# Dilated and sparse attention heads scaled one group later, the output and the mixers' rotation reordered

## The chip, the cores and the metric

One core of a Trainium2 chip runs the whole program in one launch. Its engines are TensorE (PE, with its weight loads, PEld), VectorE (DVE), ScalarE (ACT), GpSimd (POOL) and SyncE (SP), which issues the loads of the weights. The metric is the device time in microseconds, lower is better. Each time is the median of several executions.

## The reference

Two transformer stacks run one after the other on 256 tokens of width 1024, in float32. The first has two layers (the mixers, each with a feed-forward part behind it); it matters here for its rotary embedding of the grouped and the latent heads. The second has a layer with a recurrent mixer beside four sparse block heads, then a layer of eight dilated heads, each followed by an MLP. The parts that the change touches, cut short:

```python
# sparse heads (4 heads of 128, one block of 128 tokens and the selected past block)
s_own = where(causal, q k_own * Dh**-0.5, NEG);  s_sel = where(valid, q k_sel * Dh**-0.5, NEG)
p = softmax(concat([s_sel, s_own]));  out = p_sel v_sel + p_own v_own
# dilated heads (8 heads of 128, three window and stride pairs g)
s = where(mask_g, q_g k * Dh**-0.5, NEG);  lse_g = logsumexp(s)
o = sum_g softmax(lse)_g * (exp(s - lse_g) v)
x = layer_norm(alpha * x + o @ w_out)
# rotary embedding of q and k, before the scores
concat([x1 * c - x2 * s, x1 * s + x2 * c])
```

With 256 tokens all three groups of a dilated head can share one sum of exponentials: the kernel adds the three masked exponentials and multiplies by one reciprocal.

## The kernel before

**Data flow.** Weights come from memory in units of up to 128x2048 numbers. SyncE loads a unit into a ring of three (`wraw`), waiting for the low part of the unit three before. ScalarE rounds it (`split_hi`, L310, ring of four `whi`), VectorE takes the rest (`split_lo`, L318, ring of three `wlo`), and waits before it until TensorE has finished the unit three before. TensorE multiplies each block three times: high by high, high by low, low by high (L378 to L381 for a tile of a projection, 24 multiplications; L456 to L459 for row blocks). `ahead_dve` makes the splits two units ahead of TensorE, at the step where a unit begins; `ahead_act` works three ahead.

**Order.** Each engine walks the same list of steps, written out in Python, and does its own part of each step in that order. An engine never does a later step while it waits in an earlier one. So the list sets what stands behind what. Semaphores count each result.

**Attention of the dilated and the sparse heads.** A head goes through these parts: `scores` on TensorE (L2501 and L2502, or L1671 and L1672); on VectorE `masked_dve` (L917: add the mask, keep the least value); on ScalarE `scores_act` (L974: exponentials with their sums); for the dilated heads GpSimd adds the second group (`scores_pool`, L990). Then `weights_dve` on VectorE: two sums of two numbers (L942, L944), the third group's sum (L946), reciprocal (L950), scaling (L956). Two heads later TensorE transposes the weights (`headturn`, L1001), ScalarE copies them (L1011), and one more head later TensorE multiplies by the values (`values`, L1022), ScalarE and VectorE split the result (L1028, L1033). Before the change `scores_dve` does `masked_dve` and `weights_dve` in one step.

**Rotation.** For dilated and sparse heads four projected tiles are a group. ScalarE copies each tile (L848) and its 32 rotated rows (L851). TensorE permutes them (`four_pe`, L839), VectorE finishes (`four_dve`, L861, L862 and four times L867). It is called at the first tile of the next group; `qend` and `qk_end` do it for the last group. In the mixers `rot_act` swaps rows in four copies (L797) and `turn_dve` multiplies and adds (L806, L807, L810); there `rot_dve` first makes the split of tile j and then turns tile j-1.

**Steps around the heads.** `Dilated` deals its projections (`qk`, `v`) between the heads by `due`; `wo` steps are quarter row blocks of the output projection with the first four heads, six multiplications each. `Rwkv` mixes its recurrence's preparation (`prep`), late projection tiles (`z`) and the sparse heads (`att`). A z tile passes ScalarE (L1708), GpSimd (L1744) and VectorE (L1725). GpSimd also multiplies and adds the norm's gains (L723, L717) behind each of the first four dilated heads' L990.

## Time and profile before

| What | Value |
|---|---|
| Median of 3 executions | 1636.87 us (1635.64 to 1637.04) |
| The profiled execution's own time | 1636.17 us |
| Its span in the trace | 1634.4 us |
| TensorE busy | 1583.4 us, 97% |
| VectorE busy | 1113.0 us, 68% |
| ScalarE busy | 936.9 us, 57% |
| GpSimd busy | 301.2 us, 18% |
| Mixers with their feed-forward parts | 0 to about 880 us |
| Recurrent layer with the sparse heads | about 880 to 1090 us |
| Its MLP | about 1090 to 1280 us |
| Dilated heads | about 1280 to 1445 us |
| Last MLP | about 1445 us to the end |

The busy times overlap. What counts is where TensorE stands still, and what it waits for there. Rows of the timeline begin with the start in us from the span's start and the duration in us; a bracket at the end gives the engine's idle time just before and who ended it.

### The profile page before, as it was taken

The numbers are of one execution on the slowest core, as the hardware profiler recorded it, in microseconds if no ns is written. First come the engines' busy times: TensorE is split into PE (matmuls) and PEld (weight loads), VectorE is DVE, ScalarE is ACT, GpSimd is POOL, SyncE is SP. The second block draws the span as 40 slices with busy tenths as digits, with TensorE's granted clock in tenths as the row PEclk, the third lists the DMA queues.
The fourth block names the chain that finished last, engine by engine and source line by source line (L and its number), as shares of the span: only waits on it lengthen the run. The fifth ranks groups of instructions, "written<-read, shape, count | busy, mean of one in ns | idle before, by whom it ended". The sixth has DMA issues, their size and how long they took to land. (4 is left out here: it accounts for less than half of the span.)

```text
span 1634.4 us, 28813 instructions
## 1 busy us (share of the span) xinstructions
PE 1583.4 (97%) x11908; PEld 1433.5 (88%) x11908; DVE 1113.0 (68%) x1751; ACT 936.9 (57%) x1510; POOL 301.2 (18%) x218
## 2 busy tenths in 40 slices
PE   7999999999999999999999998889999999899998
PEld 6999998999899999999988986768888889878886
DVE  5575656887466665668855686579844778779744
ACT  5777755765458776556644664346533656545531
POOL 0000210433000002104320252016500021008300
PEclk9999999999999999999999999999999999999999
DMA  9344454575543534636654633025665535345651
GB/s 293 129 148 133 143 197 170 194 245 174 193 179 105 168 117 155 218 130 207 205 177 167 232 112 104 30 80 204 210 227 182 205 107 177 108 179 179 235 185 73
DMA packets 45394, 272.78 MB, mean 167 GB/s; under 512 B 4816, under 2 KB 9040, under 8 KB 16208
## 3 DMA queue, kind: packets, MB, share of 16 engines
q1 hardware_dynamic: 44544, 266.23, 47.6%
q10 hardware_dynamic: 720, 4.72, 0.8%
q8 instruction: 94, 1.54, 0.4%
q14 instruction: 36, 0.29, 0.1%
HBM read 269.88 MB, written 1.05 MB: 166 GB/s over the span
## 5 line engine op out<-in xcount | busy, mean ns | idle before, releaser
L318 DVE TENSOR_TENSOR b_wlo<-b_wraw,b_whi 128x2048 fp32r<-128x2048 f32 (+1 forms) x263 | 569.7, 2170 | 175.1 <-PE b_ps L459 125.3
L310 ACT ACTIVATE b_whi<-b_wraw 128x2048 fp32r<-128x2048 f32 (+1 forms) x263 | 467.8, 1779 | 200.0 <-PE b_ps L459 147.1
L378 PE MATMUL b_ps<-b_H,b_whi 128*128 128x256 f32 x1784 | 505.3, 283 | 0.2 <-ACT b_four L851 0.2
L380 PE MATMUL b_ps<-b_H,b_whi 128*128 128x256 f32 x1784 | 498.0, 279 | 0.0
L381 PE MATMUL b_ps<-b_H,b_wlo 128*128 128x256 f32 x1784 | 498.0, 279 | 0.0
L378 PEld LDWEIGHTS b_ps<-b_H,b_whi 128*128 128x128 f32 x1784 | 335.3, 188 | 9.4 <-issue 8.2
L380 PEld LDWEIGHTS b_ps<-b_H,b_whi 128*128 128x128 f32 x1784 | 335.5, 188 | 0.6
L381 PEld LDWEIGHTS b_ps<-b_H,b_wlo 128*128 128x128 f32 x1784 | 335.3, 188 | 0.0
L424 PE MATMUL b_ps<-b_H,b_whi 128*128 128x512 f32 x448 | 155.7, 390 | 0.0
L1550 POOL TENSOR_TENSOR b_fl<-b_ab,b_fh 128x256 fp32r<-128x256 f32 x44 | 93.7, 2129 | 213.7 <-ACT b_fh L1523 213.7
L425 PE MATMUL b_ps<-b_H,b_wlo 128*128 128x256 f32 x448 | 126.3, 282 | 0.0
L456 PE MATMUL b_ps<-b_whi,b_gh 128*128 128x512 f32 x256 | 99.7, 389 | 0.0
L459 PE MATMUL b_ps<-b_whi,b_gl 128*128 128x512 f32 x256 | 99.6, 389 | 0.0
L457 PE MATMUL b_ps<-b_wlo,b_gh 128*128 128x512 f32 x256 | 99.6, 389 | 0.0
L424 PEld LDWEIGHTS b_ps<-b_H,b_whi 128*128 128x128 f32 x448 | 84.1, 188 | 17.6
L1620 POOL TENSOR_TENSOR b_gl<-b_relu,b_gh 128x256 fp32r<-128x256 f32 x64 | 71.6, 1129 | 126.3 <-ACT b_gh L1592 126.3
L1472 POOL TENSOR_TENSOR b_mg<-b_mg,b_scr 128x256 f32<-128x256 f32 x32 | 31.5, 984 | 291.6 <-DVE b_scr L1455 291.6
L425 PEld LDWEIGHTS b_ps<-b_H,b_wlo 128*128 128x128 f32 x448 | 84.7, 189 | 0.1
L974 ACT ACTIVATE b_S<-b_S,b_small 128x256 f32<-128x256 f32 (+1 forms) x116 | 54.9, 475 | 42.1 <-DVE b_small L917 30.0
L456 PE MATMUL b_ps<-b_whi,b_H 128*128 128x512 f32 x160 | 64.8, 405 | 9.5 <-DVE b_wlo L318 6.2
L456 PE MATMUL b_ps<-b_whi,b_fh 128*128 128x512 f32 x176 | 68.7, 390 | 0.0
L459 PE MATMUL b_ps<-b_whi,b_fl 128*128 128x512 f32 x176 | 68.5, 389 | 0.0
(365 smaller groups left out, 2711.5 us busy)
## 6 DMA issues: line engine op xcount, KB each, us to landing
b_wraw<-in_w SPq DMA_DIRECT2D x223, 1024.0 KB, 4.9
b_wraw<-in_w SPq DMA_DIRECT2D x37, 512.0 KB, 3.5
b_bias<-in_rpb SPq DMA_DIRECT2D x8, 512.0 KB, 10.9
b_gains<-in_gains ACTq DMA_DIRECT2D x4, 1024.0 KB, 5.0
b_wraw<-in_w SPq DMA_DIRECT2D x2, 768.0 KB, 4.3
b_X<-in_x SPq DMA_DIRECT2D x2, 512.0 KB, 6.1
b_cA<-in_cA SPq DMA_DIRECT2D x2, 512.0 KB, 8.6
out<-b_X SPq DMA_DIRECT2D x4, 256.0 KB, 2.1
```

The lines of the kernel that those rows point to most:

```text
L310: e.activation(whi[u % NHI][:, 0:n], raw[u % NRAW][:, 0:n], ACT.Copy).then_inc(up("w_hi", "whi", u))
L318: e.tensor_tensor(wlo[u % NLO][:, 0:n], raw[u % NRAW][:, 0:n], hi.bitcast(F32), ALU.subtract).then_inc(up("w_lo", "wlo", u))
L378: e.matmul(out, wh, x.hi[:, kk, :], start=k == 0, stop=False)
L380: e.matmul(out, wh, x.lo[:, kk, :], start=False, stop=False)
L381: ins = e.matmul(out, wl, x.hi[:, kk, :], start=False, stop=last)
L424: e.matmul(bank[:, :], part(u, ng * P, k, gi * P, gi * P + P, False), H2[:, k, :, :].rearrange("p s t -> p (s t)"), start=k == 0, stop=False)
L425: ins = e.matmul(bank[:, 0:T], part(u, ng * P, k, gi * P, gi * P + P, True), x.hi[:, k, :], start=False, stop=k == job.nk - 1)
L456: e.matmul(out, xh, part(u, n, q, 0, n, False), start=k == 0, stop=False)
L457: e.matmul(out, xh, part(u, n, q, 0, n, True), start=False, stop=False)
L459: ins = e.matmul(out, xl, part(u, n, q, 0, n, False), start=False, stop=k == job.nk - 1)
L1550: e.tensor_tensor(self.f.lo[:, m, :], self.ab[p % 4][:, 0, :], self.f.hi[:, m, :].bitcast(F32), ALU.subtract).then_inc(up("f_lo", self.f.k ...
L1620: e.tensor_tensor(self.f.lo[:, j, :], self.r[p % 4][:, :], self.f.hi[:, j, :].bitcast(F32), ALU.subtract).then_inc(up("f_lo", self.f.key, ...
```

## The change

It separates `masked_dve` and `weights_dve` in the dilated and sparse heads, so that other VectorE steps stand between them. In the dilated list, `weights` stands half a head's projections later, and around head 7 the last rotation, the output steps and their splits are reordered. In the sparse part the projection tiles come in the order Q0 Q1 K0 K1 Q2 Q3 K2 K3, head 0's scores go ahead of z tile 12, the weights of a head are made in the step of the next, and the ring of score buffers starts at another buffer. In the mixers each tile is turned in its own step, so the last one (`rot` 5) ahead of the split of `vg`.

```diff
--- before.py
+++ after.py
@@ -812,8 +812,7 @@
 
     def rot_dve(e, w, job, j, tn, place):
         ahead_dve(e, w, job, j)
-        if j:
-            turn_dve(e, w, job, j - 1, tn, place)
+        turn_dve(e, w, job, j, tn, place)
 
 
 
@@ -889,10 +888,6 @@
             for what in h["needs"]:
                 w.wait_ge(*at(*what))
             h["qk"][g](e, bank).then_inc(banks.full((a.key, "s", i, g)))
-
-    def scores_dve(e, w, a, i):
-        masked_dve(e, w, a, i)
-        weights_dve(e, w, a, i)
 
     def masked_dve(e, w, a, i):
         h, k = a.heads[i], a.key
@@ -1419,10 +1414,8 @@
                     rot_dve(e, w, self.rot, *i, self.tn, self.place)
                 elif what == "vg":
                     ahead_dve(e, w, self.vg, 0)
-                    turn_dve(e, w, self.rot, 5, self.tn, self.place)
             for j in range(2):
                 rot_dve(e, w, self.uqr, j, self.tn, self.place_uq)
-            turn_dve(e, w, self.uqr, 1, self.tn, self.place_uq)
             for j in range(4):
                 ahead_dve(e, w, self.uq, j)
             for j in range(4):
@@ -1622,6 +1615,8 @@
 
 
     class Rwkv:
+        TILES = [0, 1, 4, 5, 2, 3, 6, 7]
+
         def __init__(self, key):
             H = Split(Hh, Hl, key, True)
             with ExitStack() as s1:
@@ -1635,7 +1630,7 @@
                     self.lora = sb(s2, "lora", [P, 3, 512])
                     self.mid, self.end, self.hst = sb(s2, "mid", [P, 4, 4]), sb(s2, "end", [P, 4, 4]), sb(s2, "hst", [P, 16])
                     self.cM = sb(s2, "cM", [P, sum(w for _, w in atM.values())])
-                    S_ring = [self.Z[:, 12:14, :].rearrange("p a t -> p (a t)")[:, 0:384]] + ring(s2, "S", 2, [P, 384])
+                    S_ring = ring(s2, "S", 2, [P, 384]) + [self.Z[:, 12:14, :].rearrange("p a t -> p (a t)")[:, 0:384]]
                     T_ring = [spare[:, 0:384], sb(s2, "T", [P, 384])]
                     small = sb(s2, "small", [P, 6, 12])
                     self.Q, self.K, self.V = sb(s2, "moQ", [P, 4, T]), sb(s2, "moK", [P, 4, T]), sb(s2, "moV", [P, 2, 512])
@@ -1644,7 +1639,8 @@
                         o, w = atM[name]
                         return self.cM[:, o:o + w]
 
-                    self.qk = Job("moqk", "ab_w_in_2", 0, range(8), pieces(1824, 2848), H)
+                    heads_of = pieces(1824, 2848)
+                    self.qk = Job("moqk", "ab_w_in_2", 0, range(8), [heads_of[t] for t in self.TILES], H)
                     self.tn = Gathering("moba", s2, CM("cos2"), CM("sin2"), CM("perm2"), ("cM",), scr[2:4], [self.qk])
                 with ExitStack() as s3:
                     self.BKt, self.RKB = sb(s3, "BKt", [P, 4, 512]), sb(s3, "RKB", [P, 2, 2, 4, 2, 64])
@@ -1671,19 +1667,20 @@
                     e.matmul(ps[:, 0:P], self.Q[:, h, 0:P], self.K[:, h, 0:P], start=True, stop=True)
                     return e.matmul(ps[:, P:P + T], self.Q[:, h, P:T], self.K[:, h, :], start=True, stop=True)
                 heads.append(head(qk=[qk], masks=[[cz[:, 0:P], cz[:, T:2 * T]]], widths=[P, T], tables=[("cM",)], d=P,
-                                  needs=[("rotated", "moqk", h), ("rotated", "moqk", 4 + h)],
+                                  needs=[("rotated", "moqk", self.TILES.index(h)), ("rotated", "moqk", self.TILES.index(4 + h))],
                                   v=lambda kb, h=h: self.V[:, kb, P * h:P * h + P], vneeds=[("free", ("mov", 0, tb)) for tb in range(2)], out=(self.yb, h)))
             self.moba = Attn("moba", heads, S_ring, T_ring, small)
             early = [("z", n) for n in range(7, 12)] + [("qk", j) for j in range(7)]
             self.steps = [("z", n) for n in range(7)]
             for s in range(12):
                 self.steps += [("prep", s), early[s]]
-            self.steps += [("qk", 7), ("qk_end", 7), ("prep", 12), ("z", 12), ("prep", 13), ("att", 0), ("att", 1), ("z", 13), ("att", 2), ("z", 14),
+            self.steps += [("qk", 7), ("qk_end", 7), ("prep", 12), ("att", 0), ("z", 12), ("prep", 13), ("att", 1), ("z", 13), ("att", 2), ("z", 14),
                            ("att", 3), ("prep", 14), ("att", 4), ("prep", 15), ("prep", 16), ("att", 5), ("att", 6)]
 
 
 
         def place(self, j):
+            j = self.TILES[j]
             return self.Q[:, j, :] if j < 4 else self.K[:, j - 4, :], -(128.0 ** -0.5) if j < 4 else 1.0
 
         def beside_pe(self, e, w, what, i):
@@ -1730,7 +1727,9 @@
                 four_dve(e, w, self.qk, 1, self.tn, self.place)
             else:
                 if i < 4:
-                    scores_dve(e, w, self.moba, i)
+                    masked_dve(e, w, self.moba, i)
+                if 0 <= i - 1 < 4:
+                    weights_dve(e, w, self.moba, i - 1)
                 if 0 <= i - 3 < 4:
                     values_dve(e, w, self.moba, i - 3)
 
@@ -2508,16 +2507,16 @@
             fill = [("qk", (0, j)) for j in range(16)] + [("v", (0,)), ("qend", (0,)), ("v", (1,))]
             fill += [("qk", (1, j)) for j in range(16)]
             due = [7, 11, 15, 20, 26, 30, 34, 35]
-            made, wo = due[0], 0
+            made = due[0]
             self.steps = fill[:made]
             for i in range(11):
                 if i == 7:
-                    self.steps += [("wo", (0,)), ("qend", (1,)), ("headturn", (5,)), ("values", (4,)), ("wo", (1,)), ("scores", (7,))]
-                    wo = 2
+                    self.steps += [("qend", (1,)), ("wo", (0,)), ("headturn", (5,)), ("values", (4,)), ("wo", (1,)), ("scores", (7,)), ("wo", (2,)), ("weights", (7,))]
                     continue
                 self.steps += [("scores", (i,))] if i < 8 else []
                 for late in range(2):
                     if late:
+                        self.steps += [("weights", (i,))] if i < 7 else []
                         self.steps += [("headturn", (i - 2,))] if 0 <= i - 2 < 8 else []
                         self.steps += [("values", (i - 3,))] if 0 <= i - 3 < 8 else []
                     if i < 7:
@@ -2525,8 +2524,7 @@
                         self.steps += fill[made:to]
                         made = max(made, to)
                     elif late:
-                        self.steps += [("wo", (wo,)), ("wo", (wo + 1,))]
-                        wo += 2
+                        self.steps += {8: [("wo", (n,)) for n in (3, 4, 5)], 9: [("wo", (6,)), ("wo", (7,))], 10: []}[i]
 
         def place(self, hg):
             def at_(j):
@@ -2553,7 +2551,7 @@
                     headturn_pe(e, w, self.att, *i)
                 elif what == "values":
                     values_pe(e, w, self.att, *i)
-                else:
+                elif what == "wo":
                     n, = i
                     row_pe(e, w, self.out[0], n // 4, 0, n // 2 % 2, 2 * (n % 2), 2 * (n % 2) + 2)
             banks.assign(lin=ALL, att=ALL)
@@ -2601,12 +2599,14 @@
                 elif what == "qend":
                     four_dve(e, w, self.qk[i[0]], 3, self.tn, self.place(i[0]))
                 elif what == "scores":
-                    scores_dve(e, w, self.att, *i)
+                    masked_dve(e, w, self.att, *i)
+                elif what == "weights":
+                    weights_dve(e, w, self.att, *i)
                 elif what == "values":
                     values_dve(e, w, self.att, *i)
                 elif what == "wo":
                     n, = i
-                    if n % 4 == 0:
+                    if n % 4 == 2:
                         ahead_dve(e, w, self.out[0], n // 4)
                     if n % 2:
                         res_dve(e, w, self.out[0], n // 4, n // 2 % 2, ALPHA, ("x_ready", 2))
```

`masked_dve` and `weights_dve`, `headturn` and `values` keep their bodies. `ahead_act` stays at output steps 0 and 4.

## Rows read from the trace of the kernel before

**Rows 1.** Page, part 1: busy us (share of the span) xinstructions of each engine

```profile
PE 1583.4 (97%) x11908; PEld 1433.5 (88%) x11908; DVE 1113.0 (68%) x1751; ACT 936.9 (57%) x1510; POOL 301.2 (18%) x218
```

**Rows 2.** View of waits, TensorE: us in total, times, longest us

```profile
PE b_ps L2501 <- DVE b_diK L867: 6.4, 3, 2.9
PE b_ps L1001 <- DVE b_small L917: 2.4, 1, 2.4
```

**Rows 3.** Timeline of VectorE, dilated head 0: start us, us

```profile
1309.66 0.16 DVE L942 TENSOR_TENSOR b_small<-b_small 128x2 f32<-128x2 f32 x1 [2.81 <-ACT b_S L974]
1310.77 2.73 DVE L946 TENSOR_TENSOR b_S<-b_S 128x384 f32<-128x384 f32 x1
...
1314.08 2.28 DVE L318 TENSOR_TENSOR b_wlo<-b_wraw,b_whi 128x2048 fp32r<-128x2048 f32 x1
```

**Rows 4.** Timeline of GpSimd, dilated head 0

```profile
1310.68 2.40 POOL L723 TENSOR_TENSOR b_X<-b_X,b_gains 128x1024 f32<-128x1024 f32 x1
```

**Rows 5.** Timeline of TensorE, first scores of dilated heads 1 and 2

```profile
1318.97 0.46 PE L2501 MATMUL b_ps<-b_diK,b_diQ 128*128 128x128 f32 x2 [1.26 <-DVE b_diK L867]
...
1335.17 0.46 PE L2501 MATMUL b_ps<-b_diK,b_diQ 128*128 128x128 f32 x2 [2.26 <-DVE b_diK L867]
```

**Rows 6.** Timeline of ScalarE and TensorE, permutation in dilated head 1

```profile
1326.12 0.37 ACT L851 ACTIVATE b_four<-b_ps 32x256 f32<-32x256 f32 x1
...
1326.67 0.63 PE L839 MATMUL b_ps<-b_four,b_cD 128*128 128x256 f32 x2
```

**Rows 7.** Timeline of VectorE and TensorE, value unit and scores of dilated head 3

```profile
1349.47 2.29 DVE L318 TENSOR_TENSOR b_wlo<-b_wraw,b_whi 128x2048 fp32r<-128x2048 f32 x1 [0.70 <-PE b_ps L459]
...
1354.87 0.38 PE L2501 MATMUL b_ps<-b_diK,b_diQ 128*128 128x128 f32 x2
```

**Rows 8.** Timeline of TensorE, ScalarE and VectorE, dilated heads 6 and 7

```profile
1410.24 0.40 PE L456 MATMUL b_ps<-b_whi,b_ydh 128*128 128x512 f32 x1
...
1411.13 0.37 ACT L851 ACTIVATE b_four<-b_ps 32x256 f32<-32x256 f32 x1
...
1411.33 0.56 DVE L946 TENSOR_TENSOR b_S<-b_S 128x384 f32<-128x384 f32 x1
...
1411.64 0.67 PE L839 MATMUL b_ps<-b_four,b_cD 128*128 128x256 f32 x2
...
1412.80 2.28 DVE L318 TENSOR_TENSOR b_wlo<-b_wraw,b_whi 128x2048 fp32r<-128x2048 f32 x1
...
1417.60 0.49 PE L2501 MATMUL b_ps<-b_diK,b_diQ 128*128 128x128 f32 x2 [2.89 <-DVE b_diK L867]
...
1426.78 0.52 PE L1001 MATMUL b_ps<-b_c,b_S 128*128 128x128 f32 x3 [1.52 <-DVE b_S L956]
```

**Rows 9.** Windows: us, busy PE PEld DVE ACT POOL, PEclk, DMA share, GB/s

```profile
998.00:1001.00 3.00, 1.96 (x9) 1.72 (x10) 1.79 (x7) 2.01 (x7) 0.01 (x1) 0.66 0.73 306
...
1330.00:1337.00 7.00, 4.74 (x37) 4.44 (x37) 6.82 (x10) 3.43 (x5) 0.00 (x0) 1.00 0.43 149
...
1417.50:1420.00 2.50, 2.40 (x11) 2.22 (x12) 2.21 (x10) 0.00 (x0) 0.00 (x0) 0.76 0.71 298
1420.00:1422.50 2.50, 2.50 (x12) 2.23 (x11) 0.99 (x6) 0.95 (x5) 0.00 (x0) 0.56 0.02 7
```

**Rows 10.** Timeline of ScalarE and VectorE, sparse heads

```profile
980.94 0.38 ACT L1708 ACTIVATE b_Z<-b_ps 128x256 f32<-128x256 f32 x1 [0.83 <-PE b_ps L381]
...
981.90 1.92 DVE L867 TENSOR_TENSOR b_moK<-b_four,b_scr 32x256 f32<-32x256 f32 x4
...
997.11 0.48 DVE L1725 SCALAR_TENSOR_TENSOR b_Z<-b_scr,b_par,b_Z 128x256 f32<-128x256 f32 x1 [0.50 <-POOL b_scr L1744]
```

**Rows 11.** Groups by line, shapes apart: busy us, mean ns, idle before

```profile
L797 ACT ACTIVATE b_zrot<-b_ps 32x256 f32<-32x256 f32 x64 | 24.0, 375 | 6.7 <-PE b_ps L381 6.0
```

**Rows 12.** Timeline of TensorE and VectorE, last rotations of the first mixer

```profile
99.55 1.04 PE L1001 MATMUL b_ps<-b_c,b_S 128*128 128x128 f32 x8
...
99.82 1.76 DVE L318 TENSOR_TENSOR b_wlo<-b_wraw,b_whi 128x1536 fp32r<-128x1536 f32 x1
```

## Prediction

> **What bounds the kernel now.** I read the page first. TensorE (PE) is busy for 97% of the span [rows 1], so an edit that moves work on VectorE (DVE) can gain only where PE stands still. The view of the waits, cut to PE, says where: three waits of a dilated head's scores for VectorE's rotation, 6.4 us together, and one of the sparse heads, 2.4 us [rows 2]. The timelines then give each place with its start and the idle time before it [rows 3 to 8, 10, 12], and the view by windows gives the granted clock there [rows 9]. The reader is to see that PE is full up to each wait, and that DVE is not busy all the time before it: in every head it idles 2.8 us for ScalarE's exponentials in front of L942 [rows 3]. It runs its queue in order, so the splits and the rotation that PE will ask for next stand behind that idle time. The mixers' stretch has no row in the PE waits for a rotation.
>
> **Dilated heads 0 and 1: the weights stand later.** Now, after the masks of head 0, DVE waits 2.81, scales (L942 to L956), splits (L318, 2.28 from 1314.08) and rotates [rows 3]. PE waits 1.26 for that at 1318.97, and 2.26 one head later [rows 5]. After the change the split and the rotation come first. The price of this is read from L946: 2.73 us in head 0 beside GpSimd's 2.40 us product of the gains [rows 3, 4], but 0.56 in head 6, where that product is absent [rows 8]. So an operation of DVE with two SBUF inputs waits for the whole GpSimd product. GpSimd's order doesn't change, so now the rotation meets it. The split can start when PE has finished the tile before (about 1308.8) and ends near 1311.1; the sum on GpSimd (about 1.0) and the product follow it and end near 1314.4; the rotation's SBUF part runs from there to 1316.6. PE wants it at 1317.6: the wait of 1.26 is gone, with 1.0 to spare. The scaling (1.5, below) and the next split (2.2) end near 1320.6, so the masks of head 1 start at most 0.5 earlier than now. That is the next thing late: ScalarE's copy L851 stands behind the exponentials of head 1 and releases PE's L839 at 1326.67 [rows 6]. PE, 1.4 ahead, would be there at 1325.25 and finds the copy at about 1326.0: **a new wait of 0.8**. The next rotation ends near 1331 against a demand at 1332.1, so the 2.26 go too.
>
> The Trainium skill (SBUF — State Buffer, section "SBUF: two separate sides") says that a DVE operation with two SBUF inputs and a GpSimd operation that reads SBUF exclude each other for the whole instruction; L946 agrees. It speaks against this edit, since the rotation is wanted sooner than the sum that suffers now. By it the new wait of 0.8 is there; were the rotation free of it, that wait would go and the whole would be 0.8 faster.
>
> **Dilated head 3: a new wait behind the value unit.** In the value step DVE does two splits, and the second waits for PE to finish a value unit (1349.47, idle 0.70) [rows 7]. After it now come the rotation (2.6: from 1415.0, where the split of 1412.80 ends, to PE's start at 1417.60 [rows 8]) and, 0.6 to spare, PE's scores at 1354.87 [rows 7]. After the change the scaling of head 2 stands between. It costs 1.5: 1.1 from L946 at 1411.33 to the split at 1412.80 less L1033's 0.4 [rows 8], and 0.2 for each of the two sums of two numbers when nothing blocks them (L942: 0.16 [rows 3]). This cost can't slide away, as the unit's end ties it to PE: **a new wait of 0.9**. Bounds: 0 if the split is let go earlier, 3.4 if the scaling meets the gains product (2.73 for 0.56). The product ends some 3 us before, so I take 0.9.
>
> From head 3 to 6 the rotation has room: those heads show no PE wait now, and the order gives DVE its idle 2.8 back.
>
> **Head 7: rotation ahead of the output split.** Now L318 (1412.80, 2.28) stands before the rotation and PE idles 2.89 until 1417.60 [rows 8]. The change puts the rotation first, on PE also: L839 goes ahead of the six multiplications of the first output step. Those run from 1410.24 to 1411.64, while ScalarE's last copy L851 ends at 1411.50 [rows 8]. They cover that copy now; without the cover PE waits **1.2**. Then L839, the output step and head 5 and 4 follow without a gap, and DVE rotates from 1412.8 to 1415.4, before PE is ready near 1415.8. So 2.89 go and 1.2 come. The split goes behind the masks of head 7, where DVE idled for the exponentials; its unit's consumer is the second half of the projection, over 8 us later. The DMA of weights that it releases goes some 5 us later too and still has more than 5 us until ScalarE splits it.
>
> PE also waits 1.52 for the weights of head 7 (1426.78) [rows 8]. With masks 3 us earlier and twelve more multiplications of the output before headturn 7 in PE's order, the weights are there near 1423.8, PE near 1424.1: the 1.52 go.
>
> After the wait of 2.89 the granted clock was 0.76 and then 0.56 for 2.5 us each [rows 9]: at 1.2 GHz part of the time instead of 2.4. Lost work: 0.24 x 2.5 + 0.44 x 2.5 = **1.7**. The wait of 2.26 left the clock at 1.00 (window 1330 to 1337) [rows 9], so I charge the new, shorter waits nothing. Bounds: 0 back, if the clock falls all the same; 1.7 more lost for each new wait after which it falls.
>
> **Sparse heads.** Head 0's scores move ahead of z tile 12; they need only the first rotation group, since the tiles come in the order Q0, Q1, K0, K1. That covers a PE wait of about 0.6. But ScalarE now waits for the masks of head 0, which stand behind the second rotation on DVE (L867 ends at 983.8), before it copies z tile 12. That copy now runs at 980.94 [rows 10]; it goes to about 987.3, and GpSimd's difference, DVE's L1725, the masks of head 1 and the weights of head 0 follow. The weights come near 990.1 where PE asks at 988.3: a new wait of 1.8 before headturn 0. It is hidden by the old one behind it, because head 3's masks wait for z tile 14 on ScalarE, GpSimd and DVE (L1725, 997.11) [rows 10], a chain that starts from the exponentials of head 2. Those come 0.2 earlier, as one scaling less stands ahead of the masks. The masks of head 3 then end 0.4 earlier, and the stage gains **0.3**. Bounds: 6.3 lost, if ScalarE's hold reaches the stage's end, and 2.4 gained, if the old wait [rows 2] goes whole. I take 0.3, near what the last chain gives.
>
> **Mixers.** Each of 16 rotations now waits for ScalarE's own four copies (4 x 0.375 = 1.5) [rows 11], where it used to take the tile before. I followed the DVE queue of the first layer with that wait: masks of the last pair start 1.1 later, their weights are ready near 98.5 where PE asks at 99.55, and the split at 99.82 [rows 12] goes to 102.5 and ends at 104.3, where PE wants it at 106.8. PE has no new wait: 0. The DMA behind that split goes 2.7 later and lands about when ScalarE asks. Cover gone, each would cost its 1.5. Taking the branch away costs nothing; buffer order and weight order are data only.
>
> **Sum.** Gone: 1.26 + 2.26 + 2.89 + 1.52 + 1.7 = 9.6. New: 0.8 + 0.9 + 1.2 = 2.9. One restart of PE fewer, 0.2; sparse 0.3. In all 9.6 - 2.9 + 0.5 = 7.2. The profiled execution took 1636.2 us (span 1634.4), 0.7 under the median of 1636.87: **1636.2 - 7.2 = 1629.0 us**.
>
> **Rivals.**
> 1. The loop gives nothing, head 7 alone counts. DVE's later masks feed back through ScalarE's copy, so every head of the loop shows a wait like 0.8. For: the new wait in head 1. Against: the room from head 3 on. The loop's net 3.5 - 0.8 - 0.9 = 1.8 and a little more are lost: 1631. Chance 0.14.
> 2. The rotation isn't blocked by the gains product. For: its first input sits in PSUM. Against: the other two parts read SBUF twice. 1628.2. Chance 0.06.
> 3. The clock falls after new waits, or where it fell before in the sparse stage but longer. For: after the sparse wait it was 0.66 (998 to 1001) [rows 9], and that wait was no longer than the one that kept it. 1.7 twice: 1632.4. Chance 0.08, half under the bound.
> 4. Slower: DVE held by each rotation for ScalarE's copies in the mixers, with splits late for PE. Place: rotation 0 to 5 and the two after them, in both layers; 16 x 1.5 = 24 us of holding. It decides once more than 7.2 of 24 reach PE; at half, 1636.2 - 7.2 + 12 = 1641. Against: the 1.0 and 2.5 us of room above. Chance 0.05.
> 5. No difference: ScalarE's hold in the sparse stage reaches the end, 6.3 of the 7.2. 1635.3. Against: the chain through z tile 14. Chance 0.07.
>
> **Numbers.** Mine has 0.60, by itself 1627 to 1631.5. A measurement here tells some 0.2%, 3.3 us, from no change. Faster: 0.60 + 0.14 + 0.06 and half of 3, 0.84. Within: 0.07 and the other half, 0.11. Slower 0.05. The range 1626 to 1633.5 takes in cases 1 and 2, half of 3, and a lost or doubled low clock.
>
> **What the next profile would show.** The PE waits of L2501 on L867: 6.4 us becomes about 1, at head 3 alone. New PE waits of L839 on ScalarE's L851 near heads 1 and 7. L946 takes 0.56 in all heads, and L862 or L867 of the first heads grow instead. No L1001 wait at head 7, and the clock at 1.00 there. In the sparse stage L1001 waits twice, near 1.8 and 2.5 us, and the stage ends where it did. No PE wait in the mixers. I am wrong if L946 stays at 2.7, if several heads of the loop show waits, or if the sparse stage ends over 1 us later.

## The result and the profile after

The changed kernel takes 1625.09 us (1623.29 to 1625.55, 4 executions) beside 1636.26 us of the kernel before on the same chip (4 executions). The ratio is 0.9931, with a 95% interval of 0.9917 to 0.9945. The forecast was 1629.0 and its range began at 1626.0, so the time lies just below it: 11.2 us were gained where 7.2 were forecast. The profiled execution took 1625.55 us with a span of 1623.8; against the profile before, the span is 10.6 shorter.

The page of the kernel after, part 1 (busy us, share of the span, instructions):

```profile
PE 1579.2 (97%) x11908; PEld 1430.7 (88%) x11908; DVE 1105.2 (68%) x1751; ACT 937.5 (58%) x1510; POOL 305.6 (19%) x218
```

The view of waits, TensorE, of the kernel after (us in total, times, longest). Line numbers are smaller by one to five:

```profile
PE b_ps L838 <- ACT b_four L850: 2.6, 3, 1.2
PE b_ps L996 <- DVE b_Z L951: 2.6, 1, 2.6
PE b_ps L1017 <- ACT b_T L1006: 1.8, 1, 1.8
PE b_ps L996 <- DVE b_S L951: 1.6, 1, 1.6
PE b_ps L2500 <- DVE b_diK L866: 0.8, 1, 0.8
```

Beside [rows 2]: the three waits of the scores for the rotation, 6.4 us, are one of 0.8. The sparse wait of 2.4 has become one of 2.6 with one of 1.6 ahead of it. L838 waits for ScalarE's copy three times: 0.95 ahead of the sparse heads, as in the kernel before, and 0.44 and 1.24 in the dilated heads, which are new.

Where the 10.6 us went is read from equal instructions of TensorE in both timelines: the recurrence's first (L2231, L2230) and the transposes of the norm behind the recurrence's layer and behind the dilated heads (L663). Of before:

```profile
1008.80 0.65 PE L2231 MATMUL b_ps<-b_AR,b_BH 64*64 64x64 f32 x32
...
1265.96 1.06 PE L663 MATMUL b_ps<-b_c,b_X 128*128 128x128 f32 x8 [0.37 <-DVE b_X L643]
...
1442.61 1.09 PE L663 MATMUL b_ps<-b_c,b_X 128*128 128x128 f32 x8 [0.28 <-DVE b_X L643]
```

And of after:

```profile
1007.84 0.65 PE L2230 MATMUL b_ps<-b_AR,b_BH 64*64 64x64 f32 x32
...
1263.13 1.06 PE L663 MATMUL b_ps<-b_c,b_X 128*128 128x128 f32 x8 [0.37 <-DVE b_X L643]
...
1432.01 1.11 PE L663 MATMUL b_ps<-b_c,b_X 128*128 128x128 f32 x8 [0.28 <-DVE b_X L643]
```

| Stretch | Forecast | Measured in the profiles |
|---|---|---|
| Up to the first sparse permutation (974.89 and 975.12) | 0 | 0.2 later |
| Sparse heads | 0.3 | 1.2 |
| Recurrence and its MLP | 0 | 1.9 |
| Dilated heads | 6.9 | 7.8 |

TensorE in the dilated heads of the kernel after:

```profile
1314.50 0.38 PE L2500 MATMUL b_ps<-b_diK,b_diQ 128*128 128x128 f32 x2
...
1322.67 0.67 PE L838 MATMUL b_ps<-b_four,b_cD 128*128 128x256 f32 x2 [0.44 <-ACT b_four L850]
...
1328.78 0.38 PE L2500 MATMUL b_ps<-b_diK,b_diQ 128*128 128x128 f32 x2
...
1349.31 0.46 PE L2500 MATMUL b_ps<-b_diK,b_diQ 128*128 128x128 f32 x2 [0.78 <-DVE b_diK L866]
...
1406.18 0.67 PE L838 MATMUL b_ps<-b_four,b_cD 128*128 128x256 f32 x2 [1.24 <-ACT b_four L850]
...
1410.45 0.39 PE L2500 MATMUL b_ps<-b_diK,b_diQ 128*128 128x128 f32 x2
...
1418.93 0.49 PE L996 MATMUL b_ps<-b_c,b_S 128*128 128x128 f32 x3
```

These answer to [rows 5 to 8]. The waits of 1.26, 2.26, 2.89 and 1.52 have no bracket any more. The three new ones stand where they were forecast: 0.44 for 0.8, 0.78 for 0.9, 1.24 for 1.2.

VectorE and GpSimd in head 0, after, beside [rows 3, 4]:

```profile
1309.38 2.30 DVE L861 TENSOR_TENSOR b_four<-b_four,b_cD 128x256 f32<-128x256 f32 x1
...
1313.78 0.55 DVE L941 TENSOR_TENSOR b_S<-b_S 128x384 f32<-128x384 f32 x1
```

```profile
1306.65 2.38 POOL L985 TENSOR_TENSOR b_S<-b_S 128x384 f32<-128x384 f32 x1 [123.53 <-ACT b_S L969]
1309.00 2.39 POOL L723 TENSOR_TENSOR b_X<-b_X,b_gains 128x1024 f32<-128x1024 f32 x1
```

The third group's sum is down to 0.55, and the rotation's L861, which takes 0.41 where GpSimd stands still, takes 2.30 in its place. GpSimd's own sum takes 2.38 here and 0.99 in head 1; VectorE's split (1305.87 to 1308.16) runs beside it. So each of the two engines is held by the other.

The view by windows of the kernel after (us; busy PE, PEld, DVE, ACT, POOL; granted clock; DMA share; GB/s), beside [rows 9]:

```profile
999.00:1002.00 3.00, 3.00 (x13) 2.56 (x12) 2.21 (x6) 1.36 (x4) 1.35 (x2) 0.50 0.16 68
1002.00:1005.00 3.00, 2.26 (x19) 1.99 (x17) 0.69 (x1) 2.01 (x4) 2.33 (x3) 1.00 0.00 0
...
1411.00:1414.00 3.00, 3.00 (x18) 2.57 (x17) 2.99 (x14) 0.56 (x3) 0.00 (x0) 1.00 0.00 0
```

At head 7 the clock stays at 1.00, as forecast. In the sparse stage of this profile it is back at full from 1002, where the kernel before had 0.57 over all of 998 to 1005 (how much of that belongs to the order of the steps comes below, under e2):

```profile
998.00:1005.00 7.00, 5.96 (x24) 5.25 (x25) 2.90 (x9) 3.46 (x10) 3.05 (x4) 0.57 0.31 131
```

### The profile page after: what moved, and what is told of

Read it like the earlier page. It is cut to its first block and busy times, and to the rows that moved or that the text cites. A ratio compares the mean times of both kernels' runs of the same rounds, so it can differ in the third digit from the quotient of the medians.

```text
span 1623.8 us, 28814 instructions
## 1 busy us (share of the span) xinstructions
PE 1579.2 (97%) x11908; PEld 1430.7 (88%) x11908; DVE 1105.2 (68%) x1751; ACT 937.5 (58%) x1510; POOL 305.6 (19%) x218
```

## The experiments

### The parts one by one

e1 to e4 are the kernel before with one part of the change each: only the mixers' `rot_dve`; only the class `Rwkv`; only the loop; only head 7 and the output. The expectations count each wait of TensorE some 0.15 us longer than the brackets of the profile do (1.42 for 1.26, 3.06 for 2.89). In the dilated list, e3 and e4 take back of the changed kernel, cut short:

```diff
 # e3: head 7, the output steps behind it and their splits as before, the loop's weights late
-("qend", (1,)), ("wo", (0,)), ... ("scores", (7,)), ("wo", (2,)), ("weights", (7,))
+("wo", (0,)), ("qend", (1,)), ... ("scores", (7,)), ("weights", (7,))
 # e4: the loop as before, head 7 and the output reordered
-self.steps += [("scores", (i,))] if i < 8 else []
+self.steps += [("scores", (i,)), ("weights", (i,))] if i < 7 else []
```

Expected of e1: 

> Of the four parts only the mixers' rotation stands in its tile's own step; the sparse and dilated lists are those of before. Theory (the parts add, and each gains what its own waits say): no new wait of TensorE between 0 and 880 us, start of the recurrent layer within 0.3 us of before, span 1634.4 +- 0.4, ratio 1.000. Rival (holding VectorE for ScalarE's copies does cost, and the whole kernel hides it elsewhere): some 2 to 12 us more, ratio 1.001 to 1.007.

Expected of e2: 

> Only the sparse part. Theory A (the whole 2.8 us that the kernel after has gained by 1063 us comes from the sparse part): the waits before the first headturn (1.7), before head 2's (2.6) and before values (1.9), the granted clock at half for 3.4 us and not 6.8, no issue pause of 1.4 us near 1021; the recurrence's end 2.8 earlier, span 1631.6. Theory B (only the clock and the waits are the sparse part's, -1.1, and the pause of TensorE's instruction stream near 1021 comes and goes by itself or with the addresses of the code): the pause of 1.4 may be there, span 1633.3.

Expected of e3: 

> Only the dilated loop's weights stand half a head later; head 7 and the output are ordered as before. Theory: the waits of 1.4 and 2.4 before the scores of heads 1 and 2 go, 0.6 (copy L850 in head 1) and 0.9 (scores of head 3) come: 2.3 gained in the loop. At head 7 the wait of 3.06 stays at 3 or a little less, with 1.7 behind it and the low clock: span 1632.1. Rival (the loop's room carries over to head 7): the wait there shrinks to under 2, span 1630 or less.

Expected of e4: 

> Only head 7 and the output are reordered, the weights of heads 0 to 6 stand right after their masks. Theory: the waits of 3.06 and 1.69 and the 1.7 of low clock go, 1.4 before the permutation comes: 5.0 gained, span 1629.4. Rival (the reorder needs the loop's earlier rotations: the scaling of head 6 now stands ahead of the last rotation): a wait of 0.5 to 1.5 before the scores of head 7 stays and the clock may fall: span 1630.5 to 1632.

| Kernel | Median us (executions) | Ratio to before, 95% interval | Span us |
|---|---|---|---|
| before | 1636.66 (29) | | |
| e1 mixers | 1636.14 (10) | 0.9999, 0.9989 to 1.0009 | 1637.6 |
| e2 sparse | 1634.80 (10) | 0.9993, 0.9984 to 1.0003 | 1632.8 |
| e3 loop | 1633.20 (10) | 0.9982, 0.9969 to 0.9994 | 1634.0 |
| e4 head 7 | 1630.43 (8) | 0.9965, 0.9954 to 0.9976 | 1630.1 |

The mixers' part is worth nothing, and e2's gain is not told from none by its interval. From 30 to 880 us TensorE's waits are the same two with it (e1) and without. Of e1:

```profile
PE b_ps L521 <- ACT b_spare L507: 1.5, 2, 0.8
PE b_ps L456 <- DVE b_wlo L318: 0.6, 1, 0.6
```

e2 has a pause near 1021 (1.5: TensorE stands still there with nothing to wait for; more below), as theory B had it. But its sparse stage, from the first permutation (975.02) to the recurrence's first product (1006.33), took 31.3 us after 33.9, with the clock at full all the way, so that the same order gave 2.6 here and 1.2 in the profile of after. How long this stage takes hangs on low clock that comes and goes with the same instructions. The work lost to it is the length of a stretch times one less its granted clock; over the profiles of all runs:

| Work lost in the stage, us | Order of before, us | Changed order, us |
|---|---|---|
| 3.4 | 33.8 and 33.9 (e3, before) | |
| 1.7 | 33.5 twice (e1, e4) | 32.5 to 33.0 (after, e5, e8, e13, e14, e15) |
| none | 31.9 (e10) | 31.3 to 31.4 (e2, e6, e7, e12) |

At an equal clock the changed order gains 0.5 to 1.0.

e4 came at 1630.1 for 1629.4, with low clock behind the old wait of head 2.

The order in e1's dilated heads is that of before, and yet they took 141.4 us from the first scores (1304.48) to L663 (1445.86), against 138.7 before: its waits are those of before, but it lost 5.1 us of work to low clock there and before 1.7. So a single profile misleads by up to 2.7 us here. e3 shows the same: its two waits of the loop are gone, as expected, but from those scores to L663 it gained 0.15 alone (1303.67 to 1442.24). It had two stretches of low clock (3.4 us of work lost) behind the waits at head 7, and its wait for the weights of head 7 was longer than the 1.52 of before:

```profile
1424.81 0.62 PE L997 MATMUL b_ps<-b_c,b_S 128*128 128x128 f32 x3 [2.28 <-DVE b_S L952]
```

```profile
1414.50:1418.50 4.00, 3.59 (x12) 3.21 (x13) 2.64 (x10) 0.00 (x0) 0.00 (x0) 0.57 0.51 215
1424.00:1429.00 5.00, 4.19 (x16) 3.74 (x17) 3.39 (x8) 2.68 (x3) 0.00 (x0) 0.66 0.01 3
```

Each execution comes with its mean granted clock, and the 29 executions of before beside e1 to e4 show how the time goes with it:

| Mean granted clock | Executions of before | Mean us |
|---|---|---|
| 0.997 | 4 | 1633.97 |
| 0.996, 0.995 | 6 | 1635.50 |
| 0.994 | 5 | 1636.63 |
| 0.993 | 12 | 1637.88 |
| 0.992 | 2 | 1638.57 |

A mean clock lower by a thousandth goes with 0.9 us more. The profile on which the forecast rests was at 0.995, better than the middle of these 29, but in the middle of all 66 executions of before beside the 16 runs (33 of them lie at 0.995 or above); their mean is 1636.24 us.

### The changed kernel again, and its three new waits

```diff
 # e6: the first output step ahead of the rotation
-("qend", (1,)), ("wo", (0,)), ("headturn", (5,))
+("wo", (0,)), ("qend", (1,)), ("headturn", (5,))
 # e7: the weights of head 2 behind ("qend", (0,)) and no more ahead of it
-self.steps += fill[made:to]
+part = fill[made:to]
+if late and i == 2:
+    part = [part[0], ("weights", (2,))] + part[1:]
+self.steps += part
 # e8: GpSimd's four products of the gains ahead of the heads, and none behind the sums
+for n in range(4):
+    w.wait_ge(*at("full", (self.qk[0].key, n)))
+    gains_pool(e, w, "l20", 2, n // 2, n % 2)
```

Expected of e5: 

> The changed kernel once more, unaltered, to see what of its gain belongs to one profile or to four executions. Each execution comes with its granted clock; the executions of the kernel before spread from 0.992 (1638.6 us) to 0.997 (1634.0). Theory (a part of the gain is low clock that the changed kernel no longer runs into): its executions keep to 0.996 to 0.998, median 1624 to 1626, ratio 0.9925 to 0.9940. At an equal clock of 0.997 the two kernels stand 9 us apart. Rival (the first four executions were lucky): clocks down to 0.993, median 1627 to 1629. The pause of TensorE's instruction stream of 1.4 us near 1020 us, absent from the first profile of this kernel and there in all five others: if it only comes and goes it is there now, and the span is 1.4 us more.

Expected of e6: 

> The changed kernel, but on all engines the first output step stands ahead of the last rotation again (the split of its weights stays behind the masks of head 7). Theory of the prediction (six multiplications covered ScalarE's copy, without them TensorE waits 1.2): the wait of 1.40 before the permutation goes, the scores of head 7 wait for VectorE no more than 0.5, span 1.0 to 1.4 less than the changed kernel's, ratio to before 0.9925. Rival (the rotation on VectorE then ends later by the 1.4 us of the output step, and TensorE waits for it at the scores instead): nothing gained.

Expected of e7: 

> The changed kernel, with the weights of head 2 alone moved behind the last rotation of the first four heads. Theory (the wait of 0.94 before the scores of head 3 is there because the scaling of head 2, 1.4 us, stands between the split and this rotation): the wait goes whole, span 0.9 less, headturn 2 not late. Rival (the split ahead, released by TensorE, sets this wait, not the scaling): it stays over 0.5.

Expected of e8: 

> The changed kernel, with GpSimd's four gains products (2.4 us each) ahead of the heads: each waits for one of the first four tiles and then runs beside VectorE's splits there. Theory (a VectorE operation with two SBUF inputs and a GpSimd operation wait for each other): L861 of heads 0 and 1 goes from 2.30 and 1.85 to 0.42, the masks of head 1 come 1.6 earlier, the wait of 0.60 for ScalarE's copy in head 1 goes: span 0.6 less. The splits near 1283 to 1293 may take up to 2.4 longer, hidden by VectorE's idle time there. Rival (the masks are held by TensorE's scores, and ScalarE's copy by the length of the exponentials alone): L861 shrinks but the 0.60 stays. A loss of 1 to 3 us if the first splits are late.

| Kernel | Median us | Ratio to before | From L663 near 1272 to L663 behind the heads, us |
|---|---|---|---|
| after | 1625.09 | 0.9931 | 159.05 |
| e5 after again | 1624.98 | 0.9939, 0.9925 to 0.9952 | |
| e6 | 1624.28 | 0.9934, 0.9922 to 0.9947 | 158.49 |
| e7 | 1622.93 | 0.9931, 0.9918 to 0.9943 | 158.19 |
| e8 | 1625.39 | 0.9939, 0.9926 to 0.9953 | 159.08 |

**e5** repeats the result. The nine executions of the changed kernel lie at 0.996 to 0.999 and their mean is 1624.97 us. At a clock of 0.997 five of them have a mean of 1624.91, four of before 1633.97: 9.1 us of the gain are there at an equal clock. The mean of all 66 of before lies 11.3 above that of the nine (11.7 for the 29 alone), so some 2 us of the gain go with low clock that the changed kernel no longer meets.

**e7** settles the wait at head 3: without the scaling in front the scores don't wait, and the heads gain 0.9.

```profile
1346.77 0.39 PE L2500 MATMUL b_ps<-b_diK,b_diQ 128*128 128x128 f32 x2
```

**e6** lies between its two cases: the cover takes the wait of 1.24 away, and 0.70 of it comes back at the scores, since VectorE can't end the rotation sooner.

```profile
1403.98 0.67 PE L838 MATMUL b_ps<-b_four,b_cD 128*128 128x256 f32 x2
...
1407.74 0.49 PE L2500 MATMUL b_ps<-b_diK,b_diQ 128*128 128x128 f32 x2 [0.70 <-DVE b_diK L866]
```

**e8** shows the hold between the two engines and its price. With the products gone L861 of head 0 takes 0.42, and L838 of head 1 no longer waits. The products, now beside the splits, take 4.28 and 4.45 where they had taken 2.4, and the third and fourth make the rotation ahead of head 0 late by 0.79: nothing is gained on the whole. The Trainium skill (SBUF — State Buffer, section "SBUF: two separate sides") has the shared pair as a lock for the whole instruction; e8 agrees in both directions. In order: VectorE, GpSimd, TensorE of e8.

```profile
1309.91 0.42 DVE L861 TENSOR_TENSOR b_four<-b_four,b_cD 128x256 f32<-128x256 f32 x1
```

```profile
1288.26 4.28 POOL L717 TENSOR_TENSOR b_X<-b_X,b_gains 128x1024 f32<-128x1024 f32 x1
1292.51 4.45 POOL L723 TENSOR_TENSOR b_X<-b_X,b_gains 128x1024 f32<-128x1024 f32 x1
```

```profile
1301.20 0.46 PE L2500 MATMUL b_ps<-b_diK,b_diQ 128*128 128x128 f32 x2 [0.79 <-DVE b_diK L866]
```

### The sparse stage, the pause, and a first combination

```diff
 # e9, of the changed kernel: head 0's scores back behind z tile 12
-("prep", 12), ("att", 0), ("z", 12), ("prep", 13), ("att", 1)
+("prep", 12), ("z", 12), ("prep", 13), ("att", 0), ("att", 1)
 # e10, of the kernel before: one load of weights held
+if u == 177:
+    w.wait_ge(*at("YY", 1, 0, 0))
 # e11, of the changed kernel: sparse weights right behind the masks
-if 0 <= i - 1 < 4:
-    weights_dve(e, w, self.moba, i - 1)
+    weights_dve(e, w, self.moba, i)
```

e12 is e7 with the first two products alone ahead of the heads, the first output step ahead of the rotation, the third ahead of the scores of head 7, and VectorE's splits left at their places.

Expected of e9: 

> The changed kernel, but head 0 of the sparse heads again scored behind z tile 12 and the recurrence's step. Theory of the prediction (the earlier scores cover a wait of 0.6, hold ScalarE's copy of z tile 12 from 981 to 987, and bring a wait of 1.8 before headturn 0 that the old wait behind it hides; the gain of the stage is one scaling out of the chain of head 2): the copy of z tile 12 is back at 981, the wait of 1.74 before headturn 0 is gone, one of 0.6 before L1793 is back, the wait before headturn 2 grows to about 3.5, and the recurrence starts within 0.4 of the changed kernel at the same clock. Rival (the scores' place is the gain of the stage): it starts 0.8 or more later.

Expected of e10: 

> The kernel before, with one load of weights (the one issued at 1016.55) held some 0.9 us by one more wait of SyncE. In the five profiles with a pause of 1.4 to 1.7 us in TensorE's instruction stream near 1021 (before, e1 to e4), a 16 KB transfer of the instruction queue starts only when the 1 MB load is through (1020.8 to 1021.8 beside 1017.5 to 1021.0); in the five without (the changed kernel, e5 to e8) it starts some 0.6 to 1.1 us ahead of the load. Theory (the fetch of the next instructions stood behind the load): with the load held the transfer goes ahead of it, the pause goes, the recurrence ends 1.4 earlier, span 1633.0. Rival (the pause hangs on something else, and the order of the two transfers only goes with it): it stays, span 1634.4, or the fetch that comes next is late in its place.

Expected of e11: 

> The changed kernel, but each sparse head's weights scaled right behind its masks, as before. Theory (the parting of masks and weights is what gains in the chain of the last heads, since the masks of head 3 no longer stand behind the scaling of head 2): the recurrence starts 0.4 to 1.0 later at the same clock, and the wait of 1.74 before headturn 0 shrinks, because the weights of head 0 no longer stand behind the masks of head 1. Rival (the parting does nothing, the tile order and the early scores are all of it): within 0.2.

Expected of e12: 

> The changed kernel with what the earlier runs point to: the weights of head 2 behind the last rotation (0.9), the first two gains products ahead of the heads and only these (0.6, without the wait of 0.95 that the third and fourth brought to head 0), and at head 7 the first output step ahead of the rotation and the third ahead of the scores, with VectorE's split left where it is (1.4). Theory: waits of 0.60, 0.94 and 1.40 gone and none in their place, span 2.9 under the changed kernel's, 1620.7, ratio to before 0.9915. Rival (the two products at the first tiles, or a later end of the output, give a part of it back): 1 to 2 us gained.

| Kernel | Median us | Ratio to before | Permutation to first product of the recurrence, us |
|---|---|---|---|
| before | 1635.58 (15) | | 33.91 |
| after | | | 32.72 |
| e9 | 1623.62 | 0.9922, 0.9909 to 0.9936 | 31.64 |
| e10 | 1637.97 | 1.0009, 0.9999 to 1.0018 | |
| e11 | 1626.93 | 0.9943, 0.9928 to 0.9959 | 34.27 |
| e12 | 1622.67 | 0.9921, 0.9909 to 0.9934 | |

**e9** overturns the forecast of the sparse stage: putting the scores back gains 1.1 us, where nothing was forecast. e9 lost 1.7 us of work to low clock, as after did, so the two can be compared; against all six profiles of the changed order with that loss it gains 0.9 to 1.3, and e16, with the same edit and loss, took 31.35. VectorE of before between the masks of heads 0 and 1, and the same of e9:

```profile
986.67 0.42 DVE L917 CUSTOM_DVE_ANT_0 b_Z<-b_ps,b_cM 128x256 f32<-128x256 f32 x1
...
988.81 0.28 DVE L917 CUSTOM_DVE_ANT_0 b_S<-b_ps,b_cM 128x128 f32<-128x128 f32 x1
```

```profile
986.17 0.42 DVE L912 CUSTOM_DVE_ANT_0 b_S<-b_ps,b_cM 128x256 f32<-128x256 f32 x1
986.51 0.28 DVE L912 CUSTOM_DVE_ANT_0 b_S<-b_ps,b_cM 128x128 f32<-128x128 f32 x1
...
994.85 0.48 DVE L1722 SCALAR_TENSOR_TENSOR b_Z<-b_scr,b_par,b_Z 128x256 f32<-128x256 f32 x1 [1.39 <-POOL b_scr L1743]
```

Between the two masks lay 2.1 us, in which VectorE waited for exponentials and scaled; in e9 0.3 is left, the masks' own time. Counted from the first permutation (974.89, 975.12, 974.47, 974.33), z tile 14 reaches VectorE at 22.2 in before, 21.7 in after, 20.4 in e9 and 22.6 in e11. So parting masks and weights gains 1.8, and the early scores cost 1.3 of it. With the scaling right behind the masks (e11) the early scores cost 0.3 alone, so the two parts of the edit don't simply add. The cost is the hold of ScalarE that the forecast described. The copy of z tile 12 in after, and in e9:

```profile
987.22 0.36 ACT L1705 ACTIVATE b_Z<-b_ps 128x256 f32<-128x256 f32 x1
```

```profile
980.52 0.38 ACT L1705 ACTIVATE b_Z<-b_ps 128x256 f32<-128x256 f32 x1 [0.84 <-PE b_ps L381]
```

Counted from the first permutation it comes 6.0 later, but in e9 too VectorE had no use for it until its split ended at 985.6, so that most of the 6.0 was hidden and 1.3 reached the chain. **e11** has the early scores without the parting: the stage is 1.6 longer than in after, of which 0.9 lies in the chain, the rest goes with a longer stretch of low clock (5.1 us of work lost for 1.7).

**The pause.** The recurrence's 1.9 us are for the most part one pause of TensorE's instruction stream. Of before, and of after at the same place:

```profile
1021.33 0.45 PE L1999 MATMUL b_ps<-b_XX,b_NA 64*64 64x64 f32 x12
...
1023.19 0.56 PE L1999 MATMUL b_ps<-b_XX,b_NA 64*64 64x64 f32 x20 [1.41 <-issue]
```

```profile
1020.37 0.69 PE L1998 MATMUL b_ps<-b_XX,b_NA 64*64 64x64 f32 x32
```

The packets in the traces show what goes with it. In every profile with the pause, a 16 KB transfer of the instruction queue starts when a 1 MB load of weights is nearly through or over (1020.76 beside 1017.50 to 1020.99 in before), 8.2 to 9.8 us after the transfer before it. In every one without, these transfers come 4.3 to 5.5 us apart and one stands ahead of that load (1015.43 beside 1016.53 to 1020.19 in after). The Trainium skill (Runtime: NRT & Kernel Launch, section "Instruction fetch mechanics") says that an engine's sequencer fetches its instructions in blocks of 16 KiB over a DMA queue of its own while it runs; the size agrees with the trace. **e10** is not told from before by its time, but its profile shows the place. It held the load so that it began 1.8 us behind the transposes before it instead of 1.3. The transfer did not go ahead of it: it started as the load ended, and the pause grew to 2.82.

```profile
1022.25 0.91 PE L2001 MATMUL b_ps<-b_XX,b_NA 64*64 64x64 f32 x20 [2.82 <-issue]
```

So the pause goes with the end of the load, but holding the load by this much doesn't free the transfer.

**e12** gained 1.9 in the dilated heads (129.3 us from first scores to L663, after 131.2), not 2.9: the old three waits, 2.5 together, are gone, but with one more output step ahead of the scores a wait for the weights of head 7 came:

```profile
1415.67 0.52 PE L996 MATMUL b_ps<-b_c,b_S 128*128 128x128 f32 x3 [1.00 <-DVE b_S L951]
```

### The change without one part each, and the last combination

e13, e14 and e15 are the changed kernel without the mixers', the loop's and head 7's part. e16 is e12 with e9's edit, and one more output step ahead of the headturn of head 7:

```diff
-8: [("wo", (3,)), ("wo", (4,)), ("wo", (5,))], 9: [("lo", (1,)), ("wo", (6,)), ("wo", (7,))]
+8: [("wo", (n,)) for n in (3, 4, 5, 6)], 9: [("lo", (1,)), ("wo", (7,))]
```

Expected of e13: 

> The changed kernel with the mixers' rotation as before. Theory (the mixers' part is worth nothing, before and within the whole): span 1623.8, no pause near 1020. Rival (it is the mixers' order together with the sparse order that takes the pause away): the pause of 1.4 to 1.7 is there, span 1625.3.

Expected of e14: 

> The changed kernel with the weights of dilated heads 0 to 6 right behind their masks. Theory (waits and low clock add): the waits of 1.42 and 2.42 are back, 0.60 and 0.94 go, 2.3 more; half clock for 3.4 us near 1330 to 1334 in most executions, 1.7 more: span 1626.1 or 1627.8, mean clock 0.996. Rival (the low clock has nothing to do with that wait): clock and number of low stretches as in the changed kernel.

Expected of e15: 

> The changed kernel with head 7 and the output ordered as before. Theory: the waits of 3.06 and 1.69 are back and 1.40 goes, 3.35 more; half clock for 3.4 to 6.8 us behind them, 1.7 to 3.4 more: span 1628.9 to 1630.5, executions at 0.995 to 0.996. Rival: no low clock there, 1627.1.

Expected of e16: 

> The kernel of e12 with head 0 of the sparse heads scored behind z tile 12 as in e9, and one more output step between the scores of head 7 and its headturn, where e12 had a new wait of 1.17 for the weights. Theory (e9's 1.0 to 1.6 adds to e12's, and the 1.17 goes): span 1618.0, median 1620, ratio to before 0.9900. Rival (the sparse stage's gain is given back at the low clock, or the 1.17 comes back as a wait for the last split): 1619.5 to 1620.5, no better than e12.

| Kernel | Median us | Ratio to before (1636.40, 13) | Span us | First scores to L663, us |
|---|---|---|---|---|
| e13 | 1625.67 | 0.9939, 0.9920 to 0.9957 | 1623.9 | |
| e14 | 1627.99 | 0.9948, 0.9928 to 0.9967 | 1627.5 | 135.2 |
| e15 | 1631.29 | 0.9969, 0.9959 to 0.9980 | 1630.7 | 138.4 |
| e16 | 1618.90 | 0.9895, 0.9875 to 0.9915 | 1617.2 | 128.2 |

e13 has the span of the changed kernel: the mixers' part is worth nothing in the whole either. The parts add up: the medians of e1 to e4 lie 0.5, 1.9, 3.5 and 6.2 us below that of before, 12.1 together, beside the 11.7 of the whole against the same executions, which is the same within their intervals. Without the loop's part the heads take 4.0 more: 2.3 of waits, and the low clock behind the old wait of head 2, here in e14:

```profile
1332.00:1334.00 2.00, 2.00 (x8) 1.73 (x9) 2.00 (x2) 0.00 (x0) 0.00 (x0) 0.56 0.71 299
```

Without head 7's part they take 7.2 more: the waits of 2.89 and, for the weights, 2.30 are back and the 1.24 is gone, 4.0 for the 3.35 expected, and 3.4 us of work are lost in two stretches of low clock; its ten executions lie at 0.994 to 0.996. Of the six profiles with the loop's old waits five show low clock near 1334 (e1, e2, e4, e10 and e14, but not before), of the twelve with the new ones none. With the old wait at head 7 all six show one or two stretches behind it, with the new order none.

The pause is back in e14 and in no other of these three:

```profile
1021.85 0.57 PE L1998 MATMUL b_ps<-b_XX,b_NA 64*64 64x64 f32 x21 [1.73 <-issue]
```

e14 differs from the changed kernel only in the order of steps that run some 280 us later. The pause is there in before, e1 to e4, e10 and e14, and absent wherever the sparse part and the loop's part are both in (after, e5 to e9, e11 to e13, e15, e16). So it is not the order of what has run up to there that decides; how the instructions are laid out and fetched is a guess that is left, and no run here takes that apart.

## Why the forecast was off

**Right.** The four old waits gone (7.9), three new ones in the places named (2.5 for 2.9), no wait in the mixers, the clock at 1.00 at head 7, L941 at 0.55 in all heads with L861 blocked instead, the two sparse waits (1.6 and 2.6 for 1.8 and 2.5). Rivals 1 and 2 fell: no later head shows a wait like head 1's, and the rotation is blocked. Rival 3 fell: the clock stays at 1.00 behind all new waits of the dilated heads, and the low clock of the sparse stage is no longer than before. Rival 4 fell by e1 and e13. Rival 5 named a real hold, but 1.3 of its 6.3 reached the end of the stage.

**Wrong: "I take 0.3, near what the last chain gives".** The stage gained 1.2. The forecast followed the last chain back to the exponentials of head 2 and took one scaling out of it; it didn't see that between the masks of heads 0 and 1 the scaling and VectorE's wait for the exponentials, 2.1 us, left the same chain. Its account of the hold was wrong too: the new wait at headturn 0 was hidden behind the old one, as it said, but the hold itself moved the chain by 1.3; most of its 6.0 was hidden by VectorE's split. The two errors leave 0.5 in the chain (1.8 less 1.3), and 0.5 is what the two orders differ by with no low clock (31.9 in e10, 31.3 to 31.4). So the forecast's 0.3 came near the chain's gain by luck. The rest of the 1.2 goes with the shorter low clock, of which ScalarE's copy takes a part back: L1017 waits 1.8 for it.

**Wrong: the recurrence had no term.** Its 1.9 us, most of it the pause of 1.41, are the largest single part that the forecast lacked. It put this stretch at nothing and gave no reason, though the view of waits of before has the pause as a row (TensorE, L1999, issue: 1.4). Nothing in the change touches that stage, and what took the pause away is left open above.

**Mis-sized: the low clock, "1.7" with bounds of 0 and 3.4.** The forecast read one execution and gave back what that one had lost behind head 7; between the two profiles this term came true. It charged the wait of head 2 nothing, since the clock stood at 1.00 up to 1337, where its window ended. In e1 the low clock begins at 1337, and five of six profiles with that wait show it. The dilated heads took 138.7 us in the profile of before, but 141.0 to 141.4 in the three others with their order (e1, e2, e10), against 131.1 to 131.2 in the five with the changed one (after, e5, e9, e11, e13). Over the executions the changed kernel keeps some 2 us by it. That makes the gain of the dilated heads larger than one profile shows, but it explains little of the miss, since the profile behind the forecast, with 1636.17, lay at the mean of the 66 executions. In the profiles the dilated heads gained 7.8 for 6.9; 0.4 of the difference is the smaller new waits, 0.2 lies ahead of the first scores, and the rest isn't taken apart.

With 0.9, 1.9 and 0.9 more, less the 0.2 at the start, the 7.2 become the profile's 10.6 but for rounding, and the 0.6 up to 11.2 is within the spread of the four executions (2.3).

**The better kernel.** e16 is 6.2 us below the changed kernel's median and 3.8 below e12's: no TensorE wait is left in the dilated heads, and ScalarE isn't held in the sparse stage.

## What to carry to other kernels

When a consumer of slow results (here, scaling behind exponentials) is moved behind the next independent work on an in-order engine, count the gain once for every turn of the chain, not only at its last one; and price the hold of an engine from the time at which the next engine would have been free to use its result. A forecast of under one per cent should not rest on one profile: read the spread of time against granted clock over all executions first, and ask of each wait of over 2 us in how many of them the low clock follows. Work put in front of a wait only moves it on where the engine that is waited for is itself the late one: e6 gave back 0.70 of the 1.24 that it covered, e12 1.0 of 2.5.

## What the runs showed of the hardware

- The same list of steps took 138.7 us in one profile and 141.4 in another, with the same waits but 1.7 and 5.1 us of work lost to low clock. A mean clock lower by a thousandth goes with 0.9 us more here.
- GpSimd's product of 128x1024 took 4.28 and 4.45 us beside VectorE's split of 128x2048, and 2.4 without it: GpSimd pays for the exclusion as VectorE does (0.41 becomes 2.30).
- A pause of 1.3 to 2.8 us in TensorE's instruction stream stands with a 16 KB transfer of the instruction queue that starts only as a 1 MB load of weights ends. A reordering of steps some 280 us later brought it back (e14); why is open.
